# Attention in pairs of halves, with ten gate projections held back: a hybrid decoder kernel on one core

## What is computed

```
shift, scale, gate = silu(c) @ W_ada + b_ada
h = RMSNorm(x) * (1 + scale) + shift
q, k, v, z = split(h @ w_in)             # 2048, 512, 512, 2048 columns
s = q k^T / 8 + bias                     # window 128, ALiBi
mx = max(max(s), sink)
p = exp(s - mx) / (sum exp(s - mx) + exp(sink - mx))
o = p v                                  # prompt: blocks of 128 against two key blocks
y = (o * silu(z)) @ w_out                # sample: 128 cached rows and its own 4
x = x + gate * RMSNorm(y)
```

## Time and profile before

| | us |
|---|---|
| runs, median of 3 | 2514.2 |
| runs, lowest and highest | 2513.91, 2523.45 |
| profiled execution | 2517.11 |
| its span, first to last instruction | 2515.5 |
| PE busy in the span | 2373.9 (94%) |
| DVE, ACT busy | 985.7 (39%), 683.5 (27%) |
| mean granted clock of PE | 0.943 |

### The profile page before, as it was taken

One profiled execution on the slowest core, in us unless ns is written; L12 is line 12 of the kernel. 1 busy time (PEld: TensorE's weight loads), 2 busy tenths in 40 slices (PEclk: granted clock), 3 DMA queues, 4 the chain that ended last, 5 costly groups with the idle time before them and its releaser, 6 DMA issues.

```text
span 2515.5 us, 41366 instructions
## 1 busy us (share of the span) xinstructions
PE 2373.9 (94%) x17089; PEld 2137.6 (85%) x17089; DVE 985.7 (39%) x1545; ACT 683.5 (27%) x1111; POOL 65.4 (3%) x108
## 2 busy tenths in 40 slices
PE   5779999999999899998799999999999999989996
PEld 2379989889889577776699999999999999988895
DVE  1152454453544641124654342434342434352124
ACT  1232342342332422122431222222222222232222
POOL 1000000000000000000000000000000000000000
PEclk8889999999999579998899999999999999989998
DMA  8962221312222049994456966775559556718622
GB/s 321 367 200 78 73 63 54 85 51 70 76 60 71 0 129 299 293 298 107 127 83 65 88 93 85 76 99 81 93 65 87 94 88 74 107 53 267 209 81 72
DMA packets 345768, 300.80 MB, mean 120 GB/s; under 512 B 8562, under 2 KB 287338, under 8 KB 344474
## 3 DMA queue, kind: packets, MB, share of 16 engines
q1 hardware_dynamic: 335952, 247.87, 47.2%
q0 software_dynamic: 9360, 50.19, 5.5%
q10 hardware_dynamic: 290, 0.27, 0.0%
HBM read 274.81 MB, written 27.56 MB: 120 GB/s over the span
## 4 chain that ended last, share of the span: by engine, by line
PE 89%; DMA 5%; DVE 3%; issue 2%; ACT 1%; DVEq 0%; ACTq 0%; SPq 0%
PE PJ L735 66%; DMA obuf<-in_w_ada 3%; PE MX L853 3%; PE MX L874 3%; PE MX L925 3%; PE MX L860 2%; PE MX L1052 1%; PE MX L1042 1%; DMA raw<-in_w_in_attn 1%; PE MX L1004 1%; PE MX L817 1%; PE MX L1062 1%; PE MX L835 1%; PE PJ L701 1%; DVE obuf L1534 1%
## 5 line engine op out<-in xcount | busy, mean ns | idle before, releaser
L735 PE MATMUL PJ<-h_hi,w_hi 128*128 128x272 f32 x4384 | 952.5, 299 | 43.0 <-DVE h_lo L1540 24.0
L735 PE MATMUL PJ<-h_hi,w_lo 128*128 128x272 f32 x4384 | 923.9, 293 | 0.0
L735 PE MATMUL PJ<-h_lo,w_hi 128*128 128x272 f32 x4384 | 922.6, 293 | 0.0
L735 PEld LDWEIGHTS PJ<-h_hi,w_hi 128*128 128x128 f32 x4384 | 707.3, 194 | 119.6 <-issue 98.7
L735 PEld LDWEIGHTS PJ<-h_lo,w_hi 128*128 128x128 f32 x4384 | 707.7, 194 | 0.0
L735 PEld LDWEIGHTS PJ<-h_hi,w_lo 128*128 128x128 f32 x4384 | 703.2, 194 | 0.0
L1482 DVE TENSOR_TENSOR w_lo<-raw,w_hi 128x2048 fp32r<-128x2048 f32 x106 | 243.0, 2292 | 405.3 <-ACT w_hi L1135 405.2
L1135 ACT ACTIVATE w_hi<-raw 128x2048 fp32r<-128x2048 f32 x106 | 201.9, 1904 | 17.2 <-DMA raw<-in_w_in_attn 9.2
L1229 ACT ACTIVATE arena<-arena,st 128x256 f32<-128x256 f32 x128 | 64.1, 502 | 155.3 <-DVE st L1631 155.3
L1626 DVE SCALAR_TENSOR_TENSOR arena<-arena,fix,MX 128x512 f32<-128x512 f32 x64 | 47.8, 747 | 120.3 <-PE MX L860 92.1
L1408 ACT ACTIVATE arena<-PJ 128x544 f32<-128x544 f32 x32 | 20.0, 625 | 253.0 <-PE PJ L735 253.0
(11 more groups left out here) (295 smaller groups left out, 1886.6 us busy)
## 6 DMA issues: line engine op xcount, KB each, us to landing
arena<-in_w_ada SPq DMA_DIRECT2D x64, 1024.0 KB, 5.2
raw<-in_w_in_mlstm SPq DMA_DIRECT2D x64, 1024.0 KB, 15.4
raw<-in_w_in_attn SPq DMA_DIRECT2D x40, 1024.0 KB, 5.7
obuf<-in_w_ada SPq DMA_DIRECT2D x32, 1024.0 KB, 9.8
raw<-in_w_out_attn SPq DMA_DIRECT2D x16, 1024.0 KB, 7.9
raw<-in_w_out_mlstm SPq DMA_DIRECT2D x16, 1024.0 KB, 6.2
x_spill<-arena POOLq DMA_DIRECT2D x2, 4352.0 KB, 12.6
arena<-x_spill POOLq DMA_DIRECT2D x2, 4352.0 KB, 13.7
```

The lines of the kernel that those rows point to most:

```text
L735: last = mm(PJ[:, 2 * pair + f, 0:HT], w, h[:, k, HT * f:HT * f + HT], start=(k == 0 and n == 0), stop=(k == KT - 1 and n == 2))
```

## The change

- The phases of layer 0 become three: `l0p`, the V, Q, Q, Q, Q, K of group 0; `l0`, a loop of three with Z, Z of group r and V, Q, Q, Q, Q, K of group r+1, and the attention of group r beside all eight; `l0z`, ten Z entries (blocks 12, 13, 2, 3, 6, 7, 10, 11, 14, 15), with the attention of the last group beside the first eight.
- There are 29 points, four per entry, after k = 4, 8, 11 and 15.
- `scores` and `pv` do both halves of a step pair at every second point, alternating between them; `sample_scores` alternates between column halves. `PT` becomes two tiles, the second in `misc`.
- Blocks whose gate isn't there yet (j = 2, 3) get the bare attention copied into `obuf`; a Z entry of `l0z` from the third on goes into a buffer `tz` and is multiplied into `obuf` by one more DVE step (`gated_z`). `om_done` counts 20 a group.
- The bare loop after the last entry is gone; `split_out` of all 16 rows comes after the last Z entry.
- `bias(8)` moves behind the last `om_done`.

```diff
+L0P = "VQQQQK"
+L0K = "ZZ" + L0P
+L0Z = "Z" * 10
+L0Z_BLOCKS = [12, 13, 2, 3, 6, 7, 10, 11, 14, 15]
+OM = 20
+ATT_POINTS = 29
...
+        tz = [ckT[:, 0:T], ckS[:, 0:T]]
-        PT = soft[:, 1024:1536]
+        PT = [soft[:, 1024:1536], misc[:, 0:TP]]
...
+            return 4 * e + i
...
-            bias(8)
...
+            pool.wait_ge(om_done, 1 + OM * GR)
+            bias(8)
...
+                for j in range(3):
+                    for a in range(2):
+                        ck, kk = (ckT, kT) if a == half else (ckS, kS)
+                        rhs = ck[hs, 512 * j:512 * j + 512] if j < 2 else kk[hs, P + TP:P + T]
+                        last = mm(MX[64 * a:64 * a + 64, j, 0:512 if j < 2 else TS], qS[hs, 64 * a:64 * a + 64], rhs,
+                                  start=True, stop=True)
...
+            def scores(m, y):
+                j, bp, _ = step(2 * y)
+                if y:
+                    pe.wait_ge(pmax_ready, val(0, 16, m, 2 * y))
                 for bl in range(2):
                     b = 2 * bp + bl
+                    for half in range(2):
+                        hs = slice(64 * half, 64 * half + 64)
+                        kk = kT if j // 2 == half else kS
+                        last = mm(MX[:, half, 256 * bl:256 * bl + 256], q0[hs, j, P * b:P * b + P],
+                                  kk[hs, P * b:P * b + 2 * P], start=True, stop=True)
                 last.then_inc(sc_ready, 1)
 
             def p_turn(m, x):
                 pe.wait_ge(pn_ready, val(0, 32, m, 2 * x + 2))
+                if x % 2:
+                    pe.wait_ge(pt_done, val(0, 16, m, x))
...
+            def pv(m, y):
...
+                        for half in range(2):
+                            last = mm(MX[64 * half:64 * half + 64, 3, P * bl:P * bl + P],
+                                      vtok[:, P * (b - 1 + kb) + 64 * a:P * (b - 1 + kb) + 64 * a + 64],
+                                      PT[half][:, 256 * bl + P * kb:256 * bl + P * kb + P],
+                                      start=(kb == 0 or b == 0), stop=(kb == 1))
...
+                if 14 <= p < ATT_POINTS and p % 2 == 0:
+                    pv(m, (p - 14) // 2)
+                if 10 <= p < 26 and p % 2 == 0:
+                    scores(m, (p - 10) // 2)
                 if 0 <= p - 12 < 16:
                     p_turn(m, p - 12)
...
+            POINTS = (4, 8, 11, KT - 1)
...
+            layer0("l0p", it0, None, 0)
             with pe.Fori(0, GR - 1) as r:
+                layer0("l0", (r, 0), (r, 0))
+            layer0("l0z", it0, (None, GR - 1))
...
+            for k in range(KT):
+                if k in L0Z_BLOCKS[2:]:
+                    act.wait_ge(zg_done, L0Z_BLOCKS.index(k) - 1)
+                split_out([k])
...
+                if j < 2:
+                    tt(ob, ob, MX[hs, 3, 0:256], ALU.mult).then_inc(om_done, 1)
+                else:
+                    cp(ob, MX[hs, 3, 0:256]).then_inc(om_done, 1)
...
+            def gated_z(e):
+
+                dve.wait_ge(th_done, 2 * (GR - 1) + e + 1)
+                t = tz[e % 2]
+                stt(two(t), two(t), 1.0, pj(pair_of("l0z", e)), ALU.add, ALU.mult).then_inc(freed["d"], 1)
+                dve.wait_ge(freed["d"], FREED0["d"]["l0z"] + e + 1)
+                dve.wait_ge(om_done, 1 + OM * (GR - 1 if L0Z_BLOCKS[e] < 12 else GR))
+                ob = obuf[:, L0Z_BLOCKS[e], :]
+                tt(ob, ob, t, ALU.mult).then_inc(zg_done, 1)
...
+            dve.wait_ge(zg_done, 8)
+            dve.wait_ge(om_done, 1 + OM * GR)
             dve.memset(st[:, 0:1], 0.0).then_inc(u_used, RING)
+            split_out(1, range(KT))
```

More of the change, by code:

```diff
@@ L443, in load @@
                 s = slot_of(ph, e, j)
-                if not (ph == "l0" and it[0] is None and e < 2):
+                if not (ph == "l0p" and e < 2):
                     split = fixed(sp, unit_no(ph, it, e, j - 1))
@@ L450, in load, with load_entry @@
                     .then_inc(w_in[s], 16)
-            def load_entry(it, e):
+            def load_entry(ph, it, e):
                 r, c = it
[L455 to L458, removed]
+                kinds = KINDS[ph]
+                kind, n = kinds[e], kinds[:e].count(kinds[e])
+                if ph == "l0z":
+                    block = L0Z_BLOCKS[e]
+                    src = win0[:, :, 3072 + P * block:3072 + P * block + P]
+                else:
+                    g = c if r is None else r + c
+                    if ph == "l0" and kind != "Z":
+                        g = g + 1
+                    start, per = dict(Q=(0, 512), K=(2048, 128), V=(2560, 128), Z=(3072, 512))[kind]
+                    src = win0[:, :, ds(g * per + (start + P * n), P)]
+                load(ph, it, e, 0, src)
             sp.wait_ge(c_in, 32)
@@ L472, in _ @@
                                        512 * (u // 4):512 * (u // 4) + 512]).then_inc(a0_in[u % 4], 16)
-            for e in range(2, len(L0K)):
-                load_entry((None, 0), e)
+            for e in range(2, len(L0P)):
+                load_entry("l0p", (None, 0), e)
             with sp.Fori(0, GR - 1) as r:
                 for e in range(len(L0K)):
-                    load_entry((r, 1), e)
+                    load_entry("l0", (r, 0), e)
+            for e in range(len(L0Z)):
+                load_entry("l0z", (None, 0), e)
             def out_units(ph, w, arena_free=()):
@@ L1688, in layer0 @@
+            def layer0(ph, it, m):
                 r, c = it
-                g = c if r is None else r + c
-                nz = 0
-                for e in range(len(L0K) + 1):
+                size, nz = len(KINDS[ph]), 0
+                for e in range(size + 1):
                     if e:
-                        if L0K[e - 1] == "Z":
-                            empty_z("l0", it, e - 1, g * 4 + nz, val(0, 4, it, nz + 1))
-                            nz += 1
-                        point(it, m, e - 1, 2)
-                    if e < len(L0K):
-                        split_lo("l0", it, e + 1)
-                        point(it, m, e, 0)
-                        point(it, m, e, 1)
+                        if ph == "l0z" and e > 2:
+                            gated_z(e - 1)
+                        elif KINDS[ph][e - 1] == "Z":
+                            block = L0Z_BLOCKS[nz] if ph == "l0z" else r * 4 + (4 * c + nz)
+                            nth = 2 * (GR - 1) + nz + 1 if ph == "l0z" else val(0, 2, it, nz + 1)
+                            empty_z(ph, it, e - 1, block, nth)
+                            nz += 1
+                        if m is not None:
+                            attend(m, attend_points(e - 1, 3))
+                    if e < size:
+                        split_lo(ph, it, e + 1)
+                        if m is not None:
+                            for i in range(3):
+                                attend(m, attend_points(e, i))
@@ L1702, in _ @@
             LOOP_D = 2 * (4 + 2) + 16 * (3 + 2)
-            layer0((None, 0), None)
+            layer0("l0p", it0, None)
             with dve.Fori(0, GR - 1) as r:
                 chain.enter(r, LOOP_D)
-                layer0((r, 1), (r, 0))
+                layer0("l0", (r, 0), (r, 0))
             chain.leave(GR - 1)
-            for p in range(3 * L0K.count("Z"), 28):
-                attend((None, GR - 1), p)
-                split_out(1, range(p - 12, p - 11) if p < 24 else [])
-            dve.wait_ge(om_done, 1 + 18 * GR)
+            layer0("l0z", it0, (None, GR - 1))
```

164 lines of the change are left out of this document (60 added, 104 removed).

## The result

| | before, us | after, us |
|---|---|---|
| runs, median | 2514.54 (4 runs) | 2445.39 (4 runs) |
| lowest and highest | 2513.91, 2523.45 | 2441.93, 2446.78 |
| profiled execution | 2517.11 | 2441.93 |
| its span | 2515.5 | 2440.3 |
| mean granted clock of PE | 0.943 | 0.952 |

The ratio of the times is 0.9715, with an interval of 0.9691 to 0.9739: faster by 2.8%. The forecast was 2438.5 us, with a range of 2410 to 2470; the median lies 6.9 us above the one and inside the other. The profiled executions differ by 75.2 us, the medians by 69.2: the execution shown for after was its fastest, the one for before was above its median.

The account below looks back on a forecast made before the run. PE was taken to bound the entries, a PE-DVE-ACT chain the tail. Terms after 219.40 summed to 612.7 us against 688.4 before; the 75.7 difference, off the median of 2514.2, gave 2438.5 us, range 2410 to 2470.

Parts of the forecast that it names:

- Tail and entries: Layer 0: the attention standing alone at the end, 87.2 us, goes; 34 entries after 219.40 stay at 12.00 us each.
- Points 10 to 28: Prompt attention per group: pv, scores and transposes with both halves paired cost PE 25.5 us, where 42.3 were paid.
- row halves don't overlap: Rival for the paired scores: 0.86 us more per pair, 17 us in all, 2456 us; chance 0.12.
- no overlap at all: Rival: column halves don't overlap either, 53 us in all, 2492 us, only the schedule gains; chance 0.03.
- Points 0 to 9: Sample attention per group: scores alternating between column halves leave 13.6 us of 15.4; 0.2 us of slack, no wait.
- Waits for DVE: PE waiting for softmax at points 1 and 3 of dense entries: 21.0 us in the loop, 13.4 in the last stage.
- Clock: Last stage: four 2.9 us waits each bring 3.4 us at half rate, 6.8 us in all; loop waits charged nothing.
- rival with dips in the loop: Rival: the twelve short waits in the loop lower PE's clock too, 1.7 us each, 2459 us; chance 0.10.
- Ends: Around the output product: 3.4 us of idle PE before the first split, 1.5 us from sixteen splits; back-edges 2.2 us.
- At nothing: Parts charged no time: POOL's later bias load, SP's loads, adaLN strips, and odd transposes waiting for ACT's copy.
- DVE keeps up: Rival: point 0's softmax isn't late behind the weight split; 34 us of waits and 7 of clock vanish, 2397 us; chance 0.07.
- Slower: Rival: PE stays at 1.2 GHz through the dense entries, 262 us more, 2701 us; chance 0.04.

Follow-up runs that it names:

- run 1: Changed kernel with the scores of the two row halves no longer side by side, the pv pair put between them; 2461.89 us.
- run 2: As run 1, with the pv pair taken apart too: pv half 0, scores half 0, pv half 1, scores half 1; 2485.49 us.
- run 3: Changed kernel with ACT's rounding of the next weights in layer 0 moved ahead of the last attention point; 2423.55 us, ratio 0.9624.
- run 4: As run 3, with DVE's gate step and product (gated_z) moved behind the last point of the entry; 2422.48 us, ratio 0.9625.
- run 9: Kernel of run 4 with layer 1's input weights (w_in_mlstm) declared first among the DRAM tensors; 2422.25 us, ratio 0.9628.
- run 8: Kernel before the change with 1500 already fulfilled waits added at the end of POOL's program; 2517.97 us, ratio 1.0001.

## Why the prediction was right, and where it was off

**Tail and entries** were right. The 87.2 us went, and a plain entry is 12.03 us.

**Points 10 to 28** were right, and the choice of 1.06 us for both row halves with them: run 1 gives back most of what the rival "row halves don't overlap" charges (14.8 us, where it said 17) with a quarter of the pairs left together, and run 2 37.3 us, without the samples and with some pairs left together, of the 53 of "no overlap at all". On the column halves the records of pairs start 0.01 us apart. The rule of the Trainium skill ("TensorEngine Tiling (Array Packing)", Key Properties) that tiles work in parallel is what the trace shows. Its other rule, that a change of mode drains the engine, fits the 0.2 us that run 1 gives for one more block of scores (the prediction had 0.1), though the trace can't tell a drain from another cost of getting in. The overlap outweighs it.

**Points 0 to 9** were right in size (entry 7 of the first group went from 18.74 to 17.83 us, 0.91 less, for one call). The statement that no wait would stand there was not: in the first turn PE waited 1.2 us at line 830 (old 817) for DVE's copy of the caches, where I had found 0.2 us of slack. By the prediction's own list this was a sign of being wrong. It is most of why the first turn is 1.4 us longer than the second.

**Waits for DVE** had the right place and mechanism, which run 3 shows: take the rounding out of the way, and 24.4 us of waits become 3.9. The term was too large. In the loop the wait at point 1 is 0.89 us, where I had 1.3 (1.41 in the first dense entry of a turn, where I had 1.9), the one at point 3 is 0.2, where I had 0.3, and a dense entry is 19.51, where I had 20.0. With the two back-edges that makes 425.2 us for three turns against 428.5.

**The last stage** was off by more: 175.9 us against 182.7, some 3 us of it in the waits and 4 in the clock. One step was wrong: that ahead of the softmax DVE would wait 0.62 us for the tanh. ACT and DVE of the changed kernel at the end of such an entry (the transposes of its last point start at 717.00):

```profile
717.79 0.72 DVE L1704 SCALAR_TENSOR_TENSOR arena<-arena,PJ 128x544 f32<-128x544 f32 x1
718.54 0.72 DVE L1708 TENSOR_TENSOR obuf<-obuf,arena 128x544 f32<-128x544 f32 x1
719.19 0.74 DVE L1643 SCALAR_TENSOR_TENSOR arena<-arena,fix,MX 128x512 f32<-128x512 f32 x1
...
722.17 1.90 ACT L1148 ACTIVATE w_hi<-raw 128x2048 fp32r<-128x2048 f32 x1
724.10 2.29 DVE L1497 TENSOR_TENSOR w_lo<-raw,w_hi 128x2048 fp32r<-128x2048 f32 x1 [2.14 <-ACT w_hi L1148]
726.31 0.74 DVE L1643 SCALAR_TENSOR_TENSOR arena<-arena,fix,MX 128x512 f32<-128x512 f32 x1
```

The three DVE steps stand back to back, with no wait ahead of any of them: the tanh runs while DVE still does the gate steps of the point. So the softmax starts 2.19 us after the transposes, not 2.45, and the rounding comes 1.27 us later than in the loop (5.17 against 3.90 us after the transposes), not 1.6. The rest is the same excess as in the loop. Waits at point 1 were 2.05 us in three entries and 4.08 in the first, where I had 2.9 four times and 0.6 on top, and there was none at point 3. Dense entries of 20.45 us came out, not 21.6.

**Clock.** I charged 6.8 us for four low stretches. Three pauses of 2.05 us brought none. The one of 4.08 us, at 706.18, brought one of some 7 us, at a granted clock of 0.51, the lower level, 1.2 GHz:

```profile
704.80:711.80 7.00, 5.62 (x28) 5.37 (x30) 3.80 (x15) 2.97 (x11) 0.00 (x0) 0.51 0.45 124
```

That is some 2.5 us of loss: this entry took 24.21 us, of which 4.33 are waits, and the same entry of the loop takes 17.34 without its waits. The term was more than twice too large. The rival with dips in the loop (20 us) is out: all three turns stand at 1.00.

**Ends.** The wait was right: PE waits 3.17 us for the first split, where I had 3.4. The first output entry took 13.36 us, 1.36 over a plain one, where I had 1.5, and that was luck. I had put it down to sixteen splits ahead of the next weights. But PE is busy for all of the 13.36 us, and the second output entry starts without a wait. What stretched the first is the clock, at the lower level behind that pause:

```profile
818.24:821.00 2.76, 2.76 (x12) 2.76 (x13) 2.76 (x5) 2.76 (x6) 0.00 (x0) 0.50 0.00 0
```

2.76 us at half rate are 1.38 us lost, which is all of it. By its own argument on pauses the prediction should have charged this one; it charged the splits instead.

**"At nothing".** Right for the bias load and SP's loads in layer 0. The term that was missing altogether is layer 1: I took every stage outside the change as unaltered, and it cost 15.7 us. Layer 0 with the first output entry was 10.3 us better than the sum (602.4 against 612.7), the other stages gave some 5, and layer 1 took all of that back; by the spans the gain is 75.2 us, next to the 75.7 forecast. That this is so close is luck, a meeting of two errors, and not a sign that each term held. By the medians the gain is 69.2.

**The rivals.** "DVE keeps up" was wrong for this kernel and right for the next one. It priced waits and clock at 41 us; removing the cause gave 23.6 (run 4). "Slower" did not come: of the sixteen dense entries only the one above saw the lower level.

## What to carry to other kernels

When two engines share a chain, look at what stands in queue order between the chain's links. Here one rounding of 1.9 us that could be done a few microseconds earlier, in idle time, cost 22 us, a third of what the whole restructuring brought. Cut both traces into stages and compare the stages that nobody touched: if an engine waits there for loads (7.6 us before, 33.1 after), the difference of the totals may hold a part that does not belong to the stages you edited. A second order of declaration, with both kernels, shows how much it can be: here the two kernels were 69.2 us apart with one and 83.1 with the other.

## What the hardware showed that was not expected

- Two row halves of PE work side by side fully: eight fp32 records of 256 columns on rows 0 to 63 and 64 to 127, to two banks, take 1.06 us, as four do. They need not alternate in the queue: four of one half and then four of the other took 1.07 us (run 1, point 10).
- The time of a 1 MB load in rows of 512 bytes changed with the order in which tensors are declared. Layer 1 executed the same instructions in 1019.6 to 1097.3 us over these kernels, with medians per head from 11.6 to 32.1 us; declaring a tensor of constants first cost the kernel before 73.3 us there, and in the one execution with 4000 waits behind it the layer was 77.7 us longer.
- Pauses of PE of 2.05 us, three times, did not lower the granted clock; one of 4.08 us did, for some 7 us, and so did one of 3.17 us, for some 3 us. In the kernel before one of 2.00 us had done so the earlier trace rows. The length of a pause alone does not decide: the wait of 1.2 us in the first turn of the loop left the clock at 1.00 in the changed kernel and brought it down in runs 2, 3 and 4, where that entry took 18.6 us, not 17.1; in run 9, whose layer 0 is that of run 4, it did not. At the place of the second pause of the earlier trace rows, 0.89 us there at full clock, run 8 paused for 1.20 us and had 3.4 us at 0.50 behind it. The pause of 1.2 us in the first turn and the stretch behind it, in the changed kernel and in run 3:

```profile
229.18 2.02 PE L830 MATMUL MX<-arena 64*64 64x512 f32 x12 [1.20 <-DVE arena L1679]
231.50:235.00 3.50, 3.50 (x31) 3.50 (x29) 2.98 (x5) 0.23 (x1) 0.00 (x0) 1.00 0.00 0
```

```profile
230.69 2.02 PE L830 MATMUL MX<-arena 64*64 64x512 f32 x12 [1.21 <-DVE arena L1680]
232.90:236.50 3.60, 3.60 (x18) 3.60 (x18) 3.08 (x5) 0.22 (x1) 0.00 (x0) 0.53 0.00 0
```
